# Two more ring slots in the place of x, and the last expert's rows added by TensorE, in a streaming-encoder layer

## The reference, cut to what matters

```python
def reference(x, mem, ...):
    ...
    x = x + jnp.sum(g * proj, axis=2) @ w_out[l]
    x = x + _memory_cross_attention(_rmsnorm(x, norm_mem[l]), mem_n, ...)
    x = x + _hier_moe(_rmsnorm(x, norm_ffn[l]), w_group[l], b_group[l], w_router[l], b_router[l], w1[l], w3[l], w2[l])
    return _rmsnorm(x, final_norm)
```

## Time and profile before

| | us |
|---|---|
| median of 3 runs (lowest to highest) | 1352.01 (1351.16 to 1353.69) |
| the profiled execution, its own time | 1348.63 |
| its span, first to last instruction | 1346.6 |
| mean granted TensorE clock, share of full | 0.982 |

### The profile page before, as it was taken

One profiled execution on the slowest core, in us unless ns is written; L12 is line 12 of the kernel. 1 busy time (PEld: TensorE's weight loads), 2 busy tenths in 40 slices (PEclk: granted clock), 3 DMA queues, 4 the chain that ended last, 5 costly groups with the idle time before them and its releaser, 6 DMA issues. The chain is left out here.

```text
span 1346.6 us, 15473 instructions
## 1 busy us (share of the span) xinstructions
PE 1209.3 (90%) x6094; PEld 802.2 (60%) x6094; DVE 533.8 (40%) x980; ACT 405.5 (30%) x675; POOL 94.9 (7%) x126
## 2 busy tenths in 40 slices
PE   6999999999999999999998796999787897877784
PEld 5887877686778788888887674333333333333331
DVE  5324454568767348745445656110010010000014
ACT  5234443344543442244244421121111111111112
POOL 2000000000000000000000002211111111111100
PEclk9999999999999999999999995999999999999997
DMA  7222213212022212343423645899999999999995
GB/s 275 100 89 82 95 64 104 95 64 78 32 74 92 94 71 95 117 156 102 160 68 126 277 181 206 301 411 409 416 420 415 413 393 412 418 415 417 413 410 211
DMA packets 49436, 295.25 MB, mean 219 GB/s; under 512 B 8711, under 2 KB 8983, under 8 KB 20053
## 3 DMA queue, kind: packets, MB, share of 16 engines
q1 hardware_dynamic: 40340, 273.48, 52.0%
q0 software_dynamic: 8448, 18.69, 4.2%
q10 hardware_dynamic: 576, 2.10, 0.4%
HBM read 290.21 MB, written 12.93 MB: 225 GB/s over the span
## 5 line engine op out<-in xcount | busy, mean ns | idle before, releaser
L1825 PE MATMUL e_u<-w_raw,xT 128*64 128x512 f32 x1056 | 242.5, 605 | 58.8 <-DMA w_raw<-in_w 55.8
L1825 PEld LDWEIGHTS e_u<-w_raw,xT 128*64 128x64 f32 x1056 | 81.4, 139 | 215.6 <-issue 212.0
L2166 DVE SCALAR_TENSOR_TENSOR tn<-tn,e_u 64x512 f32<-64x512 f32 x33 | 22.4, 679 | 425.2 <-ACT tn L2067 425.2
L280 DVE TENSOR_TENSOR s_lo<-s_raw,s_hi 128x2048 fp32r<-128x2048 f32 (+1 forms) x68 | 138.5, 2037 | 56.4 <-ACT s_hi L275 55.7
L275 ACT CAST s_hi<-s_raw 128x2048 fp32r<-128x2048 f32 (+1 forms) x68 | 115.9, 1705 | 111.4 <-PE pz L594 41.1
L1835 PE MATMUL e_y<-w_raw,hidT 128*64 128x512 f32 x528 | 120.6, 598 | 15.4 <-ACT hidT L2062 15.4
L562 PE MATMUL pz<-hT_hi,s_hi 128*128 128x512 f32 x288 | 115.8, 402 | 0.0
L562 PE MATMUL pz<-hT_hi,s_lo 128*128 128x512 f32 x288 | 112.4, 390 | 0.0
L562 PE MATMUL pz<-hT_lo,s_hi 128*128 128x512 f32 x288 | 112.3, 390 | 0.0
L2057 ACT COPY xT<-e_x 128x512 f32<-128x512 f32 x33 | 19.3, 585 | 304.7 <-PE e_x L1810 304.7
L578 PE MATMUL pz<-hT_hi,s_hi 128*128 128x512 f32 x256 | 102.3, 399 | 0.5
(11 more groups left out here) (378 smaller groups left out, 1876.6 us busy)
## 6 DMA issues: line engine op xcount, KB each, us to landing
w_raw<-in_w SPq DMA_DIRECT2D x192, 1024.0 KB, 27.6
s_raw<-in_w_mix SPq DMA_DIRECT2D x30, 1024.0 KB, 4.9
s_raw<-in_w_gb SPq DMA_DIRECT2D x32, 768.0 KB, 4.3
s_raw<-in_w_out_pieces SPq DMA_DIRECT2D x4, 1024.0 KB, 4.9
w_raw<-ys_scratch SPq DMA_DIRECT2D x8, 512.0 KB, 7.3
x_sb<-in_x SPq DMA_DIRECT2D x4, 512.0 KB, 4.8
rel_bias<-in_rel_tiles POOLq DMA_DIRECT2D x8, 256.0 KB, 3.1
decay<-in_decay POOLq DMA_DIRECT2D x8, 256.0 KB, 4.3
```

What stands on the lines that cost most here:

```text
L280: nc.vector.tensor_tensor(w_lo[n % 2][:, 0:w], w_raw[n % 2][:, 0:w], w_hi[n % 2][:, 0:w].bitcast(F32), ALU.subtract).then_inc(w_split, 1)
L1825: m = nc.tensor.matmul(ps_u[o][lo:lo + FIRST, :], xT[b][:, k * FIRST:(k + 1) * FIRST], raw[j][:, kk * FF:(kk + 1) * FF], start=k == 0, sto ...
L2166: nc.vector.scalar_tensor_tensor(tn[:], tn[:], 1.0, ps_u[b][0:FIRST, :], ALU.add, ALU.mult).then_inc(s_hm, 1)
```

## The change

It has three parts, and renames semaphores in the first block so that two norms share one set.

1. **Two slots more.** `DEPTH` is 20: slots 18 and 19 lie over `x_sb`. ScalarE writes each tile of x to a new `x_scratch` in DRAM (`park`), and SyncE loads pieces 18 and 19 at the start of the second block, once that has landed. After the last weights x is loaded back (`f_back`).
2. **The table of places on ScalarE's queue** (`tables_out`, between the first and the second copy to `xT`), with two more transfers that write the weights `wsel` as single words to `wsel_scratch`.
3. **The last expert's rows don't go through DRAM.** Its rows in `ys_scratch` are filled with zeros early (GpSimd, at q = 4), its tokens' weights are gathered to `w_last`, and VectorE makes `hot_last` from them, a matrix 128 x 512 that has a row's weight at its token's column. TensorE adds `hot_last` times `yo` to every tile, and now also adds x for all tiles and the other rows for tiles 2 and 3.

```diff
-        DEPTH = 18
+        RING = 18
+        X_SLOTS = T * D // PW
+        DEPTH = RING + X_SLOTS
...
+        raw_at = [ring_at + PW * 4 * place for place in PLACES] + [x_at + PW * 4 * j for j in range(X_SLOTS)]
...
+                def park(t):
+                    act.dma_start(x_dram[t * P:(t + 1) * P, :], x_sb[:, t, :]).then_inc(s_parked[t * X_SLOTS // T], 16)
...
+                for j in range(RING, DEPTH):
+                    sp.wait_ge(s_parked[j - RING], 16 * T // X_SLOTS)
+                    load_piece(sp, *ORDER[j], ORDER[j][0])
                 known = [piece for piece in FIRST_HALF[DEPTH:DEPTH + 4] if piece[0] < FIXED]
                 ring(known)
-                sp.wait_ge(s_jobs, 1)
-                sp.dma_start(jobs_dram[0:1, 0:4 * (JOBS + 1)].rearrange("o (j q) -> (o j) q", q=4),
-                             jobsi[0:JOBS + 1, :]).then_inc(s_jobs_out, 16)
-                sp.dma_start(jobs_dram[0:1, PERM_AT:PERM_AT + EXPERTS], permi[0:1, :]).then_inc(s_jobs_out, 16)
                 sp.wait_ge(s_jobs_out, 32)
...
+                for piece in OVER_X:
+                    freed(sp, *piece)
+                for t in range(T):
+                    sp.dma_start(x_sb[:, t, :], x_dram[t * P:(t + 1) * P, :]).then_inc(f_back[t], 16)
                 for piece in END:
                     freed(sp, *piece)
                 sp.dma_start(final_gain, bass.AP(a["rows"].tensor, 0, [[0, P], [1, D]])).then_inc(f_gain, 16)
+                sp.dma_start(tokens, bass.AP(a["rows"].tensor, ROWS + D, [[0, P], [1, N]])).then_inc(f_tokens, 16)
+                sp.wait_ge(f_zero, 16)
                 for b in range(2):
-                    sp.wait_ge(s_ys[b], 16 * ((TURNS + 1 - b) // 2))
+                    sp.wait_ge(s_ys[b], 16 * ((LAST + 1 - b) // 2))
...
+                    if q == LIST_AT // 2:
+                        pool.wait_ge(o_zero, 3)
+                        pool.wait_ge(f_ids, 1)
+                        pool.indirect_dma_start(ys_halves, bass.IndirectOffsetOnAxis(idy2[:, EXPERTS - 1:EXPERTS], 0),
+                                                yoo[:], None, bounds_check=last_y, oob_is_err=False).then_inc(f_zero, 16)
+                        pool.wait_ge(f_wout, 16 * 2)
+                        pool.indirect_dma_start(w_last[:], None, wsel_dram, bass.IndirectOffsetOnAxis(ids_last[:], 0),
+                                                bounds_check=last_w, oob_is_err=False).then_inc(f_w, 16)
+                        pool.wait_ge(f_zero, 16)
...
-                store(LAST)
...
+                pe.wait_ge(f_hot, 1)
+                pe.wait_ge(s_yo, TURNS)
+                for t in range(T):
+                    pe.wait_ge(f_back[t], 16)
+                    if t < 2:
+                        pe.wait_ge(f_x, t + 1)
+                    else:
+                        pe.wait_ge(f_diag, 4)
+                    o = [summed[t][:, half * FF:(half + 1) * FF] for half in range(2)]
+                    for half in range(2):
+                        nc.tensor.matmul(o[half], ident[:], x_sb[:, t, half * FF:(half + 1) * FF],
+                                         start=True, stop=False)
+                    for half in range(2):
+                        at = slice(half * FIRST, (half + 1) * FIRST)
+                        last = nc.tensor.matmul(o[half], hot_last[at, t * P:(t + 1) * P], yo[LAST % 2][at, :],
+                                                start=False, stop=t < 2)
+                    for ch in range(2 * (t >= 2)):
+                        pe.wait_ge(f_ld[ch][t], 16)
+                        for half in range(2):
+                            last = nc.tensor.matmul(o[half], weight_diag[:, t - 2, ch, :],
+                                                    y_of(t, ch)[:, half * FF:(half + 1) * FF],
+                                                    start=False, stop=ch == 1)
+                    last.then_inc(f_last, 1)
...
+                def tables_out():
+                    act.wait_ge(s_jobs, 1)
+                    act.dma_start(jobs_dram[0:1, 0:4 * (JOBS + 1)].rearrange("o (j q) -> (o j) q", q=4),
+                                  jobsi[0:JOBS + 1, :]).then_inc(s_jobs_out, 16)
+                    act.dma_start(jobs_dram[0:1, PERM_AT:PERM_AT + EXPERTS], permi[0:1, :]).then_inc(s_jobs_out, 16)
+                    for ch in range(2):
+                        act.dma_start(wsel_dram[ch * N:(ch + 1) * N, :].rearrange("(t p) o -> p (t o)", p=P),
+                                      wsel[:, ch, :], allow_slow_non_contiguous=True).then_inc(f_wout, 16)
...
+                dve.wait_ge(f_w, 16)
+                dve.wait_ge(f_tokens, 16)
+                nc.vector.tensor_scalar(hot_last[:], tokens, tok_last[:], w_last[:], ALU.is_equal, ALU.mult
+                                        ).then_inc(f_hot, 1)
...
                 sums(0)
                 sums(1)
-                scale(0)
-                sums(2)
-                for t in range(1, T):
+                for t in range(T):
                     scale(t)
```

More of the change, by code:

```diff
@@ L467, in _ @@
                     load_weights(sp, n)
-                for j in range(DEPTH):
+                for j in range(RING):
                     place_free(sp, PLACES[j])
@@ L1773, in trunk @@
                 sem("f_" + n) for n in ("x", "ss", "ms", "sq", "o", "done", "gain", "diag", "last"))
-            END = [p for p in ORDER if AT[p] >= AT[ORDER[-1]] + 1 - DEPTH][:T + 1]
+            f_ids, f_wout, f_w, f_zero, f_tokens, f_hot = (
+                sem("f_" + n) for n in ("ids", "weights_out", "weights", "zero", "tokens", "hot"))
+            f_back = [sem(f"f_back{t}") for t in range(T)]
+            LAST_IN = [p for p in ORDER if AT[p] >= AT[ORDER[-1]] + 1 - DEPTH]
+            OVER_X = [p for p in LAST_IN if SLOT[p] >= RING]
+            END = [p for p in LAST_IN if SLOT[p] < RING][:T + 2]
             def wait(eng, q, n):
@@ L2038, in _ @@
                 experts(JOB + 1, TURNS)
-                pe.wait_ge(s_hd, TURNS)
-                for half in range(2):
-                    nc.tensor.matmul(ps_u[half], ident[:], x_sb[:, T - 1, half * FF:(half + 1) * FF],
-                                     start=True, stop=False)
-                pe.wait_ge(f_diag, 2)
-                for ch in range(2):
-                    pe.wait_ge(f_ld[ch][T - 1], 16)
-                    for half in range(2):
-                        last = nc.tensor.matmul(ps_u[half], weight_diag[:, ch, :],
-                                                y_of(T - 1, ch)[:, half * FF:(half + 1) * FF],
-                                                start=False, stop=ch == 1)
-                last.then_inc(f_last, 1)
+                pe.wait_ge(f_hot, 1)
[7 more added lines that the diff above has]
+                    o = [summed[t][:, half * FF:(half + 1) * FF] for half in range(2)]
+                    for half in range(2):
+                        nc.tensor.matmul(o[half], ident[:], x_sb[:, t, half * FF:(half + 1) * FF],
[11 more added lines that the diff above has]
+                    last.then_inc(f_last, 1)
             @block.scalar
@@ L2056, in rows_in @@
                     consumed(act, q - 2, W3B)
-                    nc.scalar.copy(xT[q % 2][:], ps_x[:]).then_inc(s_xT, 1)
+                    nc.scalar.copy(xT[q % 2][:], ps_x).then_inc(s_xT, 1)
                 def hidden_in(q):
@@ L2061, in hidden_in @@
                     consumed(act, q - 2, W2B)
-                    nc.scalar.copy(hT[q % 2][:], ps_h[:]).then_inc(s_hT, 1)
+                    nc.scalar.copy(hT[q % 2][:], ps_h).then_inc(s_hT, 1)
                 def halves(q):
@@ L2094, in _ @@
                         act.wait_ge(o_tx, r + 1)
-                        nc.scalar.copy(xT[0][:], ps_x[:]).then_inc(o_xT, 1)
+                        nc.scalar.copy(xT[0][:], ps_x).then_inc(o_xT, 1)
                         act.wait_ge(o_up, r + 1)
@@ L2107, in _ @@
                 for t in range(T):
[L2108 to L2114 removed]
+                    act.wait_ge(f_last, t + 1)
+                    nc.scalar.activation(junk, summed[t][:], ACT.Square, accum_out=ss[:, t:t + 1]).then_inc(f_ss, 1)
                     act.wait_ge(f_ms, t + 1)
@@ L2218, in scale @@
                         dve.wait_ge(f_gain, 16)
-                    summed = x_sb[:, t, :] if t < T - 1 else ps_last[:]
-                    nc.vector.scalar_tensor_tensor(x_sb[:, t, :], summed, ss[:, t:t + 1], final_gain,
+                    nc.vector.scalar_tensor_tensor(x_sb[:, t, :], summed[t][:], ss[:, t:t + 1], final_gain,
                                                    ALU.mult, ALU.mult).then_inc(f_o, 1)
```

114 lines of the change are left out of this document (62 added, 52 removed).

## The result

The changed kernel takes 1365.6 us (median of 4 runs, 1362.6 to 1366.7) against 1351.6 (1350.0 to 1353.7) of the kernel before beside it. The ratio is 1.0108, 95% interval [1.0085, 1.0131]. It is 14 us slower, where the prediction had 5 us faster. The profiled execution took 1364.95 us, span 1362.9, mean granted clock 0.978.

A forecast was written before the change was run, and what follows sets the result against it. The prediction took the expert stage to be bound by DMA of the weight pieces. Tail +6 and start -11 gave -5 us: 1343.6 from the profiled 1348.6, hence a median of 1347, range 1341 to 1352.5.

The forecast's parts named there:

- The failed step: At the expert block's start: writing 1,024 single words of weights costs 0 to 1.5 us.
- the 11 us forecast for the start: Start of the weight stream: of 16.2 us missing at full speed, 11 are won; bounds 8 and 13.5.
- Rival (c): Start: the table isn't earlier, only the two pieces count, 5 us, and the tail takes them: 1353 us; chance 0.07.
- the hole of 2 us: Start: the stream's gap at 849, without a cause in the trace, was expected again and costs 2 us.
- The piece behind the table: Start: SyncE's next weight piece after the table was to be issued near 845 us, not 859.
- the pause ahead of the first freed place: Start: DMA stays idle 2.5 us between piece 19 and the first freed place.
- the table: Start: on ScalarE's queue the table of places takes 3 us and is there at 843, ending an 11.9 us wait.
- Tail: +6 forecast: After the last down products: TensorE's new products end at 1346.7 instead of 1340.45, costing 6 us; bounds +2.5 and +10.
- rival (b): Tail: the 64-row products run one behind the other, tail +9.5, sum -1.5: 1350.5 us, no change; chance 0.17.
- The lower bound of +2.5: Tail: least cost, 2.5 us, if the first pair of ys tiles lands at 1322.
- (a): Tail: milder, ys loads at 1318.1 with engines free, tail +2.5, sum -8.5: 1343.5 us; chance 0.18.
- (d): Tail: TensorE stays at 1.2 GHz, its 17.2 us become 34.4, sum +10: 1362 us; chance 0.08 with losses like it.

The follow-up runs named there:

- 32 bytes late: The changed kernel with weights sent at turn 2 as 128 runs of 32 bytes in one transfer, VectorE working out places: 1352.92 us, ratio 1.0008.
- words late: The changed kernel with ScalarE's 1,024 single words issued at turn 2 instead of ahead of the first turn: 1366.21 us, ratio 1.0114.
- slots and table: The changed kernel without the words of weights and with the tail of the kernel before: 1345.78 us, ratio 0.9962.
- table alone: The kernel before with only the table of places moved to ScalarE's queue, 18 slots: 1347.69 us, ratio 0.9985.
- scatters late: The kernel with the new order, GpSimd's eight scatters to list_scratch moved from the expert block's opening to turns 2 to 5: 1338.19 us, ratio 0.9907.
- the new order: 32 bytes late, with TensorE making x plus the last expert's rows for all tiles before the ys loads: 1342.40 us, ratio 0.9922.

## Why the prediction was wrong

**The failed step.** "1,024 single words of weights, for which no row stands, 0 to 1.5 us." They cost 13 to 14 us: after against 32 bytes late, 1.0108 - 1.0008 = 0.0100 or 13.5 us; words late against 32 bytes late, 14.3. No row bounded them from above, and 1.5 us was no bound by a row; in the 11 us forecast for the start they even stand at zero (16.2 - 2.5 - 2 - 0.6 = 11.1). Without them (32 bytes late) the time is 1352.9, just above the range. The traces agree on the place: from 842 to 872 the kernel after moves 32, 41, 323, 245 and 249 GB/s where slots and table move 111, 307, 364, 426 and 382, which is 700 GB/s less over 6 us, 10.2 us at 413. Its last down products end 10.0 us later (1325.73 against 1315.69), its block time is 10.7 us longer. The late gather and the low clock are consequences of it at the start, but the total is the same at turn 2, where neither occurs. Rival (c) had the words among its causes, as a delay of the table; the table landed in time (SyncE waited 0.3 us for it) and the pieces behind it did not.

**Start: -11 forecast, -5 measured** (0.9962) without the words. Slots and table also have a tail 1.4 us longer than before (28.4 against 27.0); their block time is 6.2 us shorter. What was right: two pieces move in the idle stretch, the table is early, and the hole of 2 us comes again (852 to 854). The piece behind the table went at 849.1, not at 845: SyncE had the table, but places came free later. The trace of slots and table has these rows, TensorE's first and last products of the block, an issue of SyncE, and two windows:

```profile
837.12 9.46 PE L1843 MATMUL e_u<-w_raw,xT 128*64 128x512 f32 x32 [0.68 <-ACT xT L2080]
...
1312.04 3.65 PE L1853 MATMUL e_y<-w_raw,hidT 128*64 128x512 f32 x16 [0.46 <-ACT hidT L2085]
```

```profile
843.17 0.80 SPq L203 DMA_DIRECT2D w_raw<-in_w  x2
```

```profile
846.00:847.00 1.00, 1.00 (x9) 0.49 (x5) 0.00 (x0) 0.00 (x0) 0.69 (x2) 1.00 0.46 106
847.00:848.00 1.00, 0.60 (x6) 0.46 (x5) 0.00 (x0) 0.00 (x0) 0.71 (x1) 1.00 0.93 393
```

Two terms were mis-sized. The first is the pause ahead of the first freed place, put at 2.5 us. It doesn't end with the issue at 843.17 but when the pieces flow, 3.8 us later: 842 to 848 loses 302 x 6 / 413 = 4.4 us. The second, larger one is the table, worth some 6 of the 11 us in the forecast by bytes. It measured 0 in the ratios beside the slots, and 2.0 us in block time; the other pairs give 3.0 (table alone), 2.2 and 1.6 to 2.0. The waits tell why it is little. With the scatters late, first the table on ScalarE, then on SyncE:

```profile
SPq L203 <- PE e_u L1844: 19.8, 5, 7.5
```

```profile
SPq L203 <- PE e_u L1844: 13.9, 4, 7.6
...
SPq L1868 <- DMA jobs_scratch<-permi: 6.7, 1, 6.7
```

What SyncE waits for the table, it no longer waits for places. By bytes, 830 to 872 gained 71 GB/s over 42 us, 7.2 us of the stream (280 against 209 GB/s), but the last down products came only 3.9 us earlier. Half of the other 3 us lies behind 872: from there to 1300 slots and table moved 176.3 MB where before had 177.0, 1.7 us. Why that is so, and the rest, stay open.

**Tail: +6 forecast, +10 in the trace after** (+6 in the ratios of 32 bytes late against slots and table, 1.0008 - 0.9962; +8 in their traces). The mechanism was right: `ys` loads hardly earlier, first sum at 8.2 us behind the last down products (7.9 forecast), TensorE alone after it. TensorE took 21.8 us instead of 19.2. Of this 0.7 is the clock: to the next group, the first two groups take 3.68 and 2.01 us, where they take 1.92 and 1.06 at the full clock, so 2.7 us are lost and 2 were forecast. Most of the rest is the change between 128-row and 64-row products: four instructions of x to the next group take 1.92 us and the last rows' 1.06, against 1.72 and 0.86 by 0.43 us each, so 0.2 us at each of eight changes, 1.6 us that the sum had left unpriced. Between groups of the same kind (line 2092 to line 2083 at 1349.21) there is no such gap. The pairs by rows do run together; rival (b) is out. The end took 7.1 us instead of 6.1; the difference is in the last store, 4.0 us from VectorE's last instruction to the end of the span against 3.1, and doesn't come again with 32 bytes late (3.1). The lower bound of +2.5 was too low by its own times: a first pair at 1322 instead of 1325 leaves +3.4.

**Sum.** In the ratios, -5 (slots and table) + 6 (tail) + 13.5 (words) = 14.5 us, measured 14.0. This is no check: each term is the difference between two versions in a chain from before to after, so they must add up. What carries the attribution is that the words moved, halved and spread changed the time as they did.

**The rivals.** (a) is out: the `ys` loads come 1.7 us behind the last down products, not earlier. (d), slower by the clock, had the sign and the wrong cause: TensorE lost 2.7 us at 1.2 GHz in its tail, not 17: after its first two groups the granted clock was 1.00 again (1340 to 1342), and the next four instructions took 1.99 us. The right slower rival, an unpriced write that holds all engines, was not on the list, though (c)'s rule of one descriptor per element pointed at it.

## What to carry to other kernels

An operation for which no row stands must be given a bound from a row, however far, before a range is closed; here a gather of 9 us beside it would have been nearer than "0 to 1.5". Single words to DRAM can be dear when they lie close together: write the tile as it lies, one run per partition, and work out the place in the reader's index, or spread the words. Look in the windows for a high DMA share at low GB/s; the dear transfers showed it each time. And when work is added to a tail, put first what needs nothing late: against the tail of slots and table (28.4 us), the new order turned +8 us into -4.6. Last, set windows of two executions side by side only after looking when the stretch opened in each.

## What the runs showed of the hardware

- 1,024 words of 4 bytes, written by ScalarE with neighbours 4 bytes apart, cost about 14 us of all DMA traffic by the ratios and 9 to 11 us in the profiled executions, half the words about half; by GpSimd 20 us (1.0156 less 1.0008). Spread, with neighbours 256 bytes apart in a filled scratch, they cost 0.9 to 1.5 us (1.0015 and 1.0019 against the 1.0008 of 128 runs, within the intervals nothing), whoever sent them. Adjacent, the sender matters: 1.0156 [1.0138, 1.0175] against 1.0114 [1.0092, 1.0137], though GpSimd's words also stood in other turns (0 to 3).
- Pairs of 64-row products on the two halves of the array run together, four instructions in 1.13 us against 1.98 for full ones; each change between the two kinds costs about 0.2 us. The Trainium skill, "TensorEngine Tiling (Array Packing)", section Key Properties, says that such a change drains TensorE; the trace agrees and gives this price.
- A 1 MB piece issued while the DMA engines stand idle doesn't flow at once. From SyncE's issue to the first microsecond at 290 GB/s or more there passed 1.8 us in before (issue 841.16; 295 GB/s from 843) and 3.8 us with slots and table (issue 843.17; 393 GB/s from 847). With the scatters late it was 2.8 and 3.3 us in two executions. What makes up the difference stays open.
